# Rotary rotation on one core: the crossed rows fetched by small transfers instead of multiplied by a permutation matrix

## The chip, the cores and the metric

One core of one Trainium2 chip runs the whole kernel in one launch. The metric is the device time of an execution in microseconds (us); lower is better. The kernel before took 1447.31 us as the median of three runs.

## The reference, cut to what matters

Two stacks are computed in fp32 for 256 tokens of width 1024: first two layers of feed-forward blocks with a recurrent and a spatial gating mixer, then two "hybrid" layers of 272 tokens (16 meta tokens ahead) with windowed attention beside an mLSTM. Only this part of the hybrid layer bears on the change:

```python
aq, ak, av, ag, mq, mk, mv, mi, mf, mo, mgate = jnp.split(h @ w_in, split_points(), axis=-1)
q = rms_norm_2(aq.reshape(B, L, 16, 64), q_norm_g)      # 16 query heads of 64
k = rms_norm_2(ak.reshape(B, L, 2, 64), k_norm_g)       # 2 key heads of 64
q, k = apply_partial_rope(q, cos, sin), apply_partial_rope(k, cos, sin)

def apply_partial_rope(x, cos, sin):                    # half = 8: 16 of the 64 channels are turned
    x1, x2, rest = x[..., :half], x[..., half:16], x[..., 16:]
    return jnp.concatenate([x1 * c - x2 * s, x2 * c + x1 * s, rest], axis=-1)
```

## The kernel before, in words

**Layout.** Activations lie with channels on the 128 partitions (rows) and tokens along the row. A tile of queries is two heads, rows 0 to 63 and 64 to 127; there are eight of them (`q`), and one tile of keys (`k_att`). The rotation crosses rows 0 to 7 of each head with its rows 8 to 15.

**Weights.** All weights are streamed once in units of 512 KB (`UNITS`). SP issues the transfer of a unit into one of four buffers `raw` (L541) once DVE has split the unit four before it; ACT rounds it into `w_hi` (L1128), DVE subtracts to get `w_lo` (L1866), and PE multiplies three ways (L691). For every fifth unit of the hybrid layers the two parts lie in `y_both` instead. ACT and DVE run four units ahead of PE there.

**The stream of a hybrid layer.** Its input products are 50 units, counted u = 0, 1, ...: kv (0, 1), mif (2, 3), aq (4 to 11), mqk (12 to 19), then mv, mo, ag, mg. Units 4 + 2i and 5 + 2i give query tiles 2i and 2i + 1. The table `VISITS` says what else belongs to a unit: PE does these steps behind the unit's products, DVE in its turn for the same unit, ahead of or behind the split of the unit four on. All of it is written out in one fixed order on each engine. ACT copies each raw query tile out of the bank (L1453) and squares it (L1464). PE then sums the squares of a head (`turn`, L924, at units 5, 6, 8, 10, 12).

**The rotation before.** POOL multiplies the raw tile by the sine table into `qs` (L1828) and by the cosine table into `qc` (L1829); both have two buffers. PE multiplies `qs` by `rot_g`, a signed permutation scaled by the norm's gains (`turned`, L934, in fp32: two passes, so two records, for one product; at units 5, 8, 10, 12, 14). DVE adds the bank and `qc` and writes the tile back in place (L2316, `q_ready`). POOL waits for that sum two tiles later. There are nine tiles in each of the two layers. The tables `cos_g` and `rot_g` are made by DVE (`tables`, L2261 to L2264) behind unit 1.

**After it.** At unit 16 PE transposes values (`kx`), and at unit 18 attention begins: PE scores a head (L994, L995) after DVE has taken the maximum of the head before it (L2358 to L2363, `s_max`), and so on for 18 items.

**Start.** SP issues four units, the meta tokens, and then one small transfer for each parameter vector (L530, L534), before the loop that issues unit 4 and on. PE waits for these parameters (`par_loaded`) behind its fourth unit.

```python
for _c in range(9):
    VISITS[5 if _c == 0 else 6 + 2 * ((_c - 1) // 2)].append(("turn", _c))
for _c in range(9):
    VISITS[5 if _c == 0 else 8 + 2 * ((_c - 1) // 2)].append(("turned", _c))
```

## Time and profile before

| | us |
|---|---|
| runs, median (lowest to highest) of three | 1447.31 (1446.77 to 1447.53) |
| profiled execution, its own time | 1446.78 |
| its span | 1445.0 |
| busy in the span: PE, DVE, ACT, POOL | 1429.0, 1094.9, 853.8, 272.9 |
| first hybrid layer, kv to mqk | about 909 to 981 |
| second hybrid layer, kv to mqk | about 1178 to 1247 |

The profile is one execution. Times of events are us from the span's start. Busy time says that an engine had an instruction in it; the matmuls are pipelined and their ends are modelled, so intervals between starts are used for PE. The chain of waits goes back from the last instruction, at each step to what released it or to the instruction before it on its engine.

### The profile page before, as it was taken

To read this page: it belongs to the slowest core of one execution; us is meant where nothing else is said; L and a number is where in the kernel's file an instruction comes from. 1 tells how busy PE (TensorE), PEld (TensorE's weight loads), DVE (VectorE), ACT (ScalarE), POOL (GpSimd) and SP (SyncE) were. 2 spreads that over 40 slices of the span, in tenths; PEclk is the share of its full clock that TensorE was granted. 3 is DMA by queue.
4 is the path that set the end of the run, shared out by engine and by line. 5 is a ranking of instruction groups with operands and counts; after the bars stand their busy time and mean duration, and the time that the engine had idled before them with its cause. 6 is when DMAs were issued, how large, how long until landed. Compare 5 with 4: busy or idle time off the path is not lost.

```text
span 1445.0 us, 27301 instructions
## 1 busy us (share of the span) xinstructions
PE 1429.0 (99%) x9633; PEld 1318.0 (91%) x9633; DVE 1094.9 (76%) x2031; ACT 853.8 (59%) x1559; POOL 272.9 (19%) x329
## 2 busy tenths in 40 slices
PE   8999999999999999999999999999999999999998
PEld 7888899988888888889988888999999999999998
DVE  6777679877766777667787766798878779986883
ACT  6665458766544656446566655656757555576762
POOL 1111113121102111014031113332250035121000
PEclk9999999999999999999999999999999999999999
DMA  6667754556655666565456655554344555434533
GB/s 213 197 193 211 234 179 132 183 182 202 183 190 182 190 188 195 183 196 169 155 171 201 186 189 173 163 144 126 92 125 137 171 148 160 126 102 122 148 116 121
DMA packets 247876, 241.25 MB, mean 167 GB/s; under 512 B 15457, under 2 KB 246737, under 8 KB 247785
## 3 DMA queue, kind: packets, MB, share of 16 engines
q1 hardware_dynamic: 244888, 236.73, 53.6%
q10 hardware_dynamic: 2896, 3.30, 0.8%
q8 instruction: 58, 0.95, 0.3%
q14 instruction: 34, 0.27, 0.1%
HBM read 238.92 MB, written 1.07 MB: 166 GB/s over the span
## 4 chain that ended last, share of the span: by engine, by line
PE 79%; DVE 13%; ACT 5%; issue 2%; DMA 1%; ACTq 0%; SPq 0%; DVEq 0%
PE bank L691 72%; DVE w_lo L1866 3%; ACT w_hi L1128 1%; DVE work L2474 1%; DVE work L2423 1%; DVE work L1903 1%; PE bank L1011 1%; DVE y_both L1866 1%; PE bank L995 1%; ACT L1160 1%; DMA raw<-in_ffn_w_in_dram 1%; DVE work L2497 1%; PE bank L978 1%; PE bank L1012 0%; PE bank L994 0%
## 5 line engine op out<-in xcount | busy, mean ns | idle before, releaser
L691 PE MATMUL bank<-x_both,w_hi 128*128 128x512 f32 (+2 forms) x3216 | 747.5, 336 | 1.3 <-DVE w_lo L1866 0.8
L1866 DVE TENSOR_TENSOR w_lo<-raw,w_hi 128x1024 fp32r<-128x1024 f32 (+1 forms) x429 | 519.4, 1234 | 203.2 <-ACT w_hi L1128 202.2
L1128 ACT CAST w_hi<-raw 128x1024 fp32r<-128x1024 f32 (+1 forms) x429 | 429.4, 1028 | 125.2 <-PE bank L691 108.0
L691 PEld LDWEIGHTS bank<-x_both,w_hi 128*128 128x128 f32 x3216 | 467.5, 189 | 4.1 <-DVE w_lo L1866 1.6
L691 PEld LDWEIGHTS bank<-x_both,w_lo 128*128 128x128 f32 x2312 | 405.6, 188 | 62.5
L691 PE MATMUL bank<-x_both,w_lo 128*128 128x256 f32 (+1 forms) x2312 | 461.9, 281 | 0.0
L691 PE MATMUL bank<-y_both,w_hi 128*128 128x512 f32 (+2 forms) x1376 | 331.5, 342 | 1.6 <-DVE w_lo L1866 1.0
L691 PEld LDWEIGHTS bank<-y_both,w_lo 128*128 128x128 f32 x1040 | 184.3, 188 | 31.3
L691 PE MATMUL bank<-y_both,w_lo 128*128 128x256 f32 (+1 forms) x1040 | 206.1, 280 | 0.0
L691 PEld LDWEIGHTS bank<-y_both,w_hi 128*128 128x128 f32 x1376 | 200.2, 189 | 2.5 <-DVE w_lo L1866 1.4
L1753 POOL TENSOR_TENSOR work<-work,rstd 128x256 f32<-128x256 f32 x88 | 66.9, 782 | 412.7 <-ACT work L1197 412.7
L1179 ACT COPY pre<-bank 128x256 f32<-128x256 f32 x176 | 56.9, 375 | 67.1 <-PE bank L691 66.9
L1209 ACT CAST y_both<-work 128x256 f32 (+1 forms) x88 | 32.7, 406 | 59.5 <-DVE work L1934 59.4
L691 PE MATMUL bank<-x_both,y_both 128*128 128x272 f32 (+1 forms) x504 | 67.6, 290 | 0.0
L1197 ACT ACTIVATE work<-work 128x256 f32<-128x256 f32 x88 | 33.2, 418 | 53.3 <-DVE work L1923 53.3
L691 PEld LDWEIGHTS bank<-x_both,y_both 128*128 128x128 f32 x504 | 63.6, 188 | 0.6
L1139 ACT ACTIVATE x_both<-h,par 128x256 fp32r<-128x256 f32 (+1 forms) x56 | 28.2, 514 | 60.6 <-DVE h L1979 52.9
L1814 POOL TENSOR_SCALAR work<-work 128x256 f32<-128x256 f32 x32 | 36.3, 1135 | 95.6 <-DVE work L2391 95.6
L1718 POOL TENSOR_TENSOR sq<-h 128x256 f32<-128x256 f32 (+1 forms) x34 | 21.4, 629 | 163.2 <-DVE h L1979 162.9
L1883 DVE SCALAR_TENSOR_TENSOR x_both<-h,par,x_both 128x256 fp32r<-128x256 f32 (+1 forms) x56 | 29.1, 529 | 24.8 <-ACT x_both L1139 24.7
L1941 DVE TENSOR_TENSOR y_both<-work,y_both 128x256 f32 (+1 forms) x88 | 33.6, 423 | 15.3 <-ACT y_both L1209 14.7
L1903 DVE TENSOR_TENSOR work<-bank,rstd 128x256 f32<-128x256 f32 (+1 forms) x98 | 37.5, 422 | 4.5 <-PE bank L691 4.2
(312 smaller groups left out, 1395.7 us busy)
## 6 DMA issues: line engine op xcount, KB each, us to landing
raw<-in_ffn_w_in_dram SPq DMA_DIRECT2D x176, 512.0 KB, 3.8
raw<-in_w_in_dram SPq DMA_DIRECT2D x100, 512.0 KB, 3.7
raw<-in_ffn_w_out_dram SPq DMA_DIRECT2D x64, 512.0 KB, 4.6
raw<-in_w_out_dram SPq DMA_DIRECT2D x32, 512.0 KB, 4.5
raw<-in_ffn_w_out_dram SPq DMA_DIRECT2D x32, 384.0 KB, 3.4
raw<-in_rec_w_in_dram SPq DMA_DIRECT2D x16, 512.0 KB, 4.3
raw<-in_sg_w_in_dram SPq DMA_DIRECT2D x16, 512.0 KB, 4.3
raw<-in_rec_w_out_dram SPq DMA_DIRECT2D x8, 512.0 KB, 3.5
```

The lines of the kernel that those rows point to most:

```text
L691: i_ = mm(accs[m][:, cols], w[:, j, m * P:(m + 1) * P], moving, start=begin and g == 0 and not residual, stop=final)
L1128: nc.scalar.copy(hi_part(U)[:, 0:n, :], raw[:, s, 0:n, :]).then_inc(hi_made, 1)
L1139: i_ = activation(xview(dst, k, N), src, ACT.Copy, scale=scale)
L1179: nc.scalar.copy(ffn_b[:, m, :], bank[b][:, SEQ:2 * SEQ]).then_inc(low_copied, 1)
L1197: activation(ffn_s[:, m, :], ffn_t[:, m, :], ACT.Silu).then_inc(silu_done, 1)
L1209: nc.scalar.copy(dst, ffn_h[:, m, :]).then_inc(act_hi, 1)
L1753: TT(ffn_r[:, m, :], ffn_s[:, m, :], rstd[:, META:L], MUL).then_inc(gate_scaled, 1)
L1814: TS(pr[:, P:AW], pr[:, P:AW], rec[:, 1:2], None, MUL).then_inc(s_prob, 1)
L1866: TT(lo_part(U)[:, 0:n, :], raw[:, s, 0:n, :], hi_part(U)[:, 0:n, :].bitcast(fp32), SUB).then_inc(lo_made, 1)
L1883: i_ = STT(out=xview(dst_lo, k, N), in0=src, scalar=scale, in1=hi, op0=MUL, op1=SUB)
L1903: TT(dst, tile(pr, m, N), rstd[:, T0:L], MUL).then_inc(tile_read, 1)
L1941: TT(lo, ffn_h[:, m, :], hi.bitcast(fp32), SUB).then_inc(act_ready, 1)
```

## The change

PE's product with `rot_g` is gone, and so is `rot_g` (and the constant `rot`). The crossed rows come from transfers inside SBUF: SP copies rows 8 to 15 of each head onto rows 0 to 7 of another tile, and rows 0 to 7 onto rows 8 to 15. That takes four transfers for the key tile and four for each pair of query tiles, 20 in a layer. They stand in SP's queue ahead of the weight loads of units 9, 13, 15, 17 and 19 (`CROSS_AT`), each set behind a wait until ACT has read the tiles out. The targets are buffers that are free at that time (`mv` for queries, the last tile of `qk` for keys). POOL waits for the four transfers and multiplies the crossed tile by `sin_g`, a table of 272 columns which has the sign and the crossed gains in it; DVE's sum takes both operands from SBUF and waits for POOL. The crossed gains come by six more parameter transfers at the start.

```diff
-WORK_SLOTS = 67
+WORK_SLOTS = 69
...
-            c["sin"][h0 + k:h0 + k + half] = np.sin(ang)
+            c["sin"][h0 + k:h0 + k + half] = np.sin(ang) * (1 if k else -1)
...
+CROSS_AT = {9: 4, 13: 0, 15: 1, 17: 2, 19: 3}
...
-        rot_g = region(2, P)
+        sin_g = region(2)
...
+        crossed_k, crossed_q = qk[:, NC8 - 1, :], mv
...
+                half = ROT // 2
+                for n, src in (("attn_q_crossed", attn_q_norm_g_2), ("attn_k_crossed", attn_k_norm_g_2)):
+                    t, r, k = PAR[n]
+                    both = par_rows[r:r + k, t, :].rearrange("l (e d) -> l e d", e=2)
+                    for a, b, w in ((0, half, half), (half, 0, half), (ROT, ROT, DH - ROT)):
+                        g = src[:, b:b + w].rearrange("l (o d) -> l o d", o=1).broadcast_to((k, 2, w))
+                        sp.dma_start(both[:, :, a:a + w], g).then_inc(par_loaded, 16)
...
+            def cross(l, i):
+
+                half, T0 = ROT // 2, META if l == DEPTH - 1 else 0
+                cols = slice(2 * i, 2 * i + 2)
+                src, dst = (k_att, crossed_k) if i == 4 else (q[:, cols, T0:L], crossed_q[:, cols, T0:L])
+                sp.wait_ge(tile_read, 2 * PHASES[f"kv{l}"][1] + 1 if i == 4 else 2 * (PHASES[f"aq{l}"][1] + i) + 2)
+                for a in (0, DH):
+                    for x, y in ((a, a + half), (a + half, a)):
+                        sp.dma_start(dst[x:x + half], src[y:y + half]).then_inc(crossed[i], 16)
...
+                        if src == "w_in_2" and U - PHASES[f"kv{l}"][0] in CROSS_AT:
+                            cross(l, CROSS_AT[U - PHASES[f"kv{l}"][0]])
...
-                pe.wait_ge(par_loaded, 16 * 17)
+                pe.wait_ge(par_loaded, 16 * 23)
...
-                def turned(c):
-
-                    n = 9 * l + c
-                    pe.wait_ge(qc_new, n + 1)
-                    pe.wait_ge(cos_ready, l + 1)
-                    if c >= 2:
-                        pe.wait_ge(q_ready, n - 1)
-                    mm(bank[5 + n % 2][:, 0:L], rot_g[:, 0 if c else 1, :], qs[:, n % 2, :], start=True,
-                       stop=True).then_inc(rot_mm, 1)
...
-                do = dict(turn=turn, turned=turned, rt=rt, kx=lambda n: kx(), att=att,
+                do = dict(turn=turn, turned=lambda n: None, rt=rt, kx=lambda n: kx(), att=att,
...
-                    TT(qs[:, n % 2, :], src, cst("sin"), MUL)
+                    pool.wait_ge(crossed[(c - 1) // 2 if c else 4], 64 * (l + 1))
+                    TT(qs[:, n % 2, :], crossed_q[:, c - 1, :] if c else crossed_k, sin_g[:, 0 if c else 1, :], MUL)
...
-                    TS(rot_g[:, 0, :], cst("rot"), gq, sc, MUL, MUL)
-                    TS(rot_g[:, 1, :], cst("rot"), gk, None, MUL).then_inc(cos_ready, 1)
+                    TS(sin_g[:, 0, :], cst("sin"), pcol("attn_q_crossed", l), sc, MUL, MUL)
+                    TS(sin_g[:, 1, :], cst("sin"), pcol("attn_k_crossed", l), None, MUL).then_inc(cos_ready, 1)
...
-                    dve.wait_ge(rot_mm, n + 1)
-                    TT(dst, bank[5 + n % 2][:, 0:L], qc[:, n % 2, :], ADD).then_inc(q_ready, 1)
+                    dve.wait_ge(qc_new, n + 1)
+                    TT(dst, qs[:, n % 2, :], qc[:, n % 2, :], ADD).then_inc(q_ready, 1)
```

PE's queue behind unit 8 of the first hybrid layer, before (L924 sums the squares of a head, L934 is the product with `rot_g`, L691 the products of the next unit):

```order
L924 MATMUL bank<-con,work 128x2 [waits qsq_new]
L924 MATMUL bank<-con,work 128x2
L924 MATMUL bank<-con,work 80x2
L934 MATMUL bank<-work 128x272 [waits cos_ready,qc_new]
L934 MATMUL bank<-work 128x272 [waits q_ready,cos_ready,qc_new]
L691 MATMUL bank<-x_both,y_both 128x272 [waits lo_made]
```

and the same place now (the same lines have other numbers in the changed file, L944 and L711):

```order
L944 MATMUL bank<-con,work 128x2 [waits qsq_new]
L944 MATMUL bank<-con,work 128x2
L944 MATMUL bank<-con,work 80x2
L711 MATMUL bank<-x_both,y_both 128x272 [waits lo_made]
L711 MATMUL bank<-x_both,y_both 128x272 x23
```

Two products and their three kinds of waits have gone from between the sums and the next unit; nothing has come in their place.

SP's queue in the first hybrid layer now, from unit 4's load on (L549 are weight loads, L576 the crossing transfers; before, there were weight loads alone):

```order
L549 DMA raw<-in_w_in_dram 128x4x256 [waits lo_made] x5
L576 DMA work<-work 8x272 [waits tile_read]
L576 DMA work<-work 8x272 x3
L549 DMA raw<-in_w_in_dram 128x4x256 [waits lo_made] x4
L576 DMA work<-work 8x544 [waits tile_read]
L576 DMA work<-work 8x544 x3
L549 DMA raw<-in_w_in_dram 128x4x256 [waits lo_made] x2
L576 DMA work<-work 8x544 [waits tile_read]
L576 DMA work<-work 8x544 x3
L549 DMA raw<-in_w_in_dram 128x4x256 [waits lo_made] x2
```

Each set of four, and its wait for ACT's reading of the tiles, now stands ahead of a weight load.

DVE's queue in its turn for units 7 and 8 of the first hybrid layer, now (L1877 is the split, L2045 a 4-row step of the gates, L2327 the sum that was L2316 and waited for `rot_mm`):

```order
L2045 SCALAR_TENSOR_TENSOR work<-work 4x272 [waits dch] x3
L1877 TENSOR_TENSOR w_lo<-raw,w_hi 128x1024 [waits hi_made,dch]
L2327 TENSOR_TENSOR work<-work 128x272 [waits qc_new] x2
L1877 TENSOR_TENSOR w_lo<-raw,w_hi 128x1024 [waits hi_made]
L2045 SCALAR_TENSOR_TENSOR work<-work 4x272
```

Nothing has moved here; the sums read `work` alone where they read a bank and `work`, and wait for POOL in place of PE.

## Rows read from the trace of the kernel before

**Rows 1.** The page's busy time of each engine.

```profile
PE 1429.0 (99%) x9633; PEld 1318.0 (91%) x9633; DVE 1094.9 (76%) x2031; ACT 853.8 (59%) x1559; POOL 272.9 (19%) x329
```

**Rows 2.** Timeline of PE: start, length, line, shape, count; around two steps behind a unit.

```profile
931.70 0.75 PE L691 MATMUL bank<-x_both,w_hi 128*128 128x272 f32 x4
932.29 0.42 PE L691 MATMUL bank<-x_both,w_lo 128*128 128x272 f32 x2
...
1221.19 1.16 PE L934 MATMUL bank<-work 128*128 128x272 f32 x4
...
1222.70 0.42 PE L691 MATMUL bank<-x_both,w_lo 128*128 128x272 f32 x2
```

**Rows 3.** Chain of waits, first hybrid layer: start, length, what.

```profile
917.55 1.86 DVE rstd L1888
...
995.61 0.49 PE bank L994 x2
```

**Rows 4.** Chain of waits, second hybrid layer.

```profile
1232.83 0.45 DVE pre L1903
...
1261.69 0.49 PE bank L994 x2
```

**Rows 5.** DVE's waits for PE, 1182 to 1262: us in total, times, longest.

```profile
DVE pre L1903 <- PE bank L691: 0.7, 2, 0.4
...
DVE work L2316 <- PE bank L934: 0.4, 1, 0.4
```

**Rows 6.** Timeline of DVE: the tables, one of 272 and one of 128 columns.

```profile
920.06 0.36 DVE L2262 TENSOR_SCALAR work<-con,par 128x272 f32<-128x272 f32 x1
...
920.53 0.28 DVE L2264 TENSOR_SCALAR work<-con,par 128x128 f32<-128x128 f32 x1
```

**Rows 7.** By source line, 913 to 975 (split) and 900 to 1000 (sum): ns min/median/max.

```profile
L1866 DVE TENSOR_TENSOR w_lo<-raw,w_hi x15: 1204/1224/1693, 914.2 to 974.6; 128x1024 fp32r<-128x1024 f32 x15
...
L2316 DVE TENSOR_TENSOR work<-bank,work x9: 420/433/441, 934.7 to 965.3; 128x272 f32<-128x272 f32 x9
```

**Rows 8.** The start: SP, ACT, DVE and PE's timelines, and two answers on transfers.

```profile
13.21 0.55 SPq L534 DMA_DIRECT2D par_rows<-in_attn_k_norm_g_dram  x2
14.14 45.41 SPq L541 DMA_DIRECT2D raw<-in_ffn_w_in_dram  x18
...
DMA to landing us min/median/max: 3.6/3.6/3.6
...
L569 SPq DMA_DIRECT2D sink_tail<-in_attn_sink_dram x32: 341/484/1406, 127.2 to 166.8; - x32
...
16.34 2.94 ACT L1128 CAST w_hi<-raw 128x1024 fp32r<-128x1024 f32 x3
...
24.30 0.75 DVE L1918 TENSOR_TENSOR work<-bank,pre 128x256 f32<-128x256 f32 x2
...
25.73 0.70 PE L691 MATMUL bank<-x_both,w_hi 128*128 128x512 f32 x2
```

**Rows 9.** First hybrid layer: first pair read, loads landing (927 to 932), POOL's products, first sums.

```profile
928.58 0.79 ACT L1453 COPY work<-bank 128x272 f32<-128x272 f32 x2
...
DMA to landing us min/median/max: 3.6/4.3/4.6
...
L1828 POOL TENSOR_TENSOR work<-work,con x9: 662/672/1515, 922.1 to 959.1; 128x272 f32<-128x272 f32 x9
...
L1829 POOL TENSOR_TENSOR work<-work x9: 769/1737/1753, 923.6 to 959.7; 128x272 f32<-128x272 f32 x9
...
941.37 0.78 DVE L2316 TENSOR_TENSOR work<-bank,work 128x272 f32<-128x272 f32 x2
```

**Rows 10.** Timelines around the load of unit 19: issue, last pair read, its cast.

```profile
950.70 0.37 SPq L541 DMA_DIRECT2D raw<-in_w_in_dram  x1
...
951.15 0.81 ACT L1453 COPY work<-bank 128x272 f32<-128x272 f32 x2 [3.93 <-PE bank L691]
...
962.93 1.04 ACT L1128 CAST y_both<-raw 128x1024 fp32r<-128x1024 f32 x1
```

More of the change, by code:

```diff
@@ L36 @@
 C_AQ, C_KV, C_AG, C_MQK, C_MV, C_MIF, C_MO, C_MG = 0, 1024, 1280, 2304, 3328, 4352, 4360, 5384
-CONST_W = dict(ident=P, tri=P, amask=AW, tmask=L, mmask=P, rot=P, head_mean=2, cos=L, sin=L, k_rows=P, tail_rows=P, tail_head=ATT_H)
+CONST_W = dict(ident=P, tri=P, amask=AW, tmask=L, mmask=P, head_mean=2, cos=L, sin=L, k_rows=P, tail_rows=P, tail_head=ATT_H)
 CONST_AT = {}
@@ L61, in constants @@
     half = ROT // 2
-    for h0 in (0, DH):
-        for d in range(half):
-            c["rot"][h0 + half + d, h0 + d] = -1
-            c["rot"][h0 + d, h0 + half + d] = 1
     c["head_mean"][i, i // DH] = 1.0 / DH
@@ L87 @@
     [("norm_g_2", 16), ("mlstm_conv_w_2", 64), ("mlstm_conv_b_2", 16), ("mlstm_out_norm_g_2", 16),
-     ("attn_q_norm_g_2", 2), ("attn_k_norm_g_2", 2)],
+     ("attn_q_norm_g_2", 2), ("attn_k_norm_g_2", 2), ("attn_q_crossed", 2), ("attn_k_crossed", 2)],
 ]):
@@ L444, in build_stack @@
             sem(n) for n in ("ws_tr", "ws_read", "vt_tr", "vt_read", "sg_mm", "sg_read"))
-        cos_ready, qsq_new, qc_new, turn_mm, rot_mm, q_ready = (
-            sem(n) for n in ("cos_ready", "qsq_new", "qc_new", "turn_mm", "rot_mm", "q_ready"))
+        cos_ready, qsq_new, qc_new, turn_mm, q_ready = (
+            sem(n) for n in ("cos_ready", "qsq_new", "qc_new", "turn_mm", "q_ready"))
+        crossed = [sem(f"crossed{i}") for i in range(5)]
         rs_new, rt_mm, rt_read, k_ready, tail_new = (
```

## The prediction, on record before the changed kernel ran

> **What bounds the kernel now.** I read the busy table first: PE is busy for 99% of the span, DVE for 76% [rows 1]. By that table alone every microsecond taken off PE would come off the kernel. PE's waits are short everywhere, so the table can't tell whether PE is the bound or only never idle; the chain of waits can. In the first hybrid layer the chain is on DVE from 917.55 (the reciprocal) to 995.61, where it goes over to PE's score product L994 [rows 3]. Between these two rows stand 113 pieces of DVE, 19 of ACT and its queue, and none of PE. DVE works almost without a gap there: splits, gates, convolution, rotation sums. PE has split units ready ahead of it, so it is always busy too, but what it does has no bearing on DVE's next step. At 995.61 it has caught up and waits for DVE's maximum. All nine rotation products of that layer lie inside this stretch.
>
> In the second hybrid layer it is otherwise. The chain is on PE until about 1232.8, and on DVE and ACT from there to 1261.69, where it goes over to L994 again [rows 4]. Ahead of 1232.8 DVE is almost as full as in the first layer: its waits for PE between 1182 and 1262 are three, 0.7 us before two convolution steps and 0.4 us before one rotation sum [rows 5]. These 1.1 us are all that DVE can be ahead of its old time when PE comes sooner. Behind them PE waits for DVE.
>
> **What PE loses.** Without rotation products the first two tiles' products of a unit take 0.59 us from the first L691 behind L924 (931.70) to the first w_lo product (932.29). With two rotation products ahead it is 1.51 us from 1221.19 to 1222.70 [rows 2]. Two products cost 0.92 us, one 0.46. 18 products are 8.3 us of PE's time, 4.1 in each layer.
>
> **What comes of it.** In the first layer: nothing. The products lie beside DVE's full stretch [rows 3], DVE waits for none of them, and PE would reach the first score up to 4.1 us sooner and wait there for DVE. What is late next is what was late before, DVE. In the second layer: 1.1 us, DVE's own waits for PE [rows 5]. The bounds are 0 (other waits take their place) and 4.1 (all of it). I take 1.1, since each of the waits is on a PE step that comes sooner, and nothing beyond them can make a full DVE faster.
>
> **What DVE gets.** The tables: two of 128 columns become 272 wide, 0.36 against 0.28 us [rows 6]. That is 0.16 us a layer on the engine that is the bound, +0.3 in all. The sums: same shape, both operands in SBUF. In nine samples the sum from a bank took 420 to 441 ns, while the split, whose two operands lie in SBUF, took from 1204 to 1693 ns [rows 7]; the long ones stand where POOL was at its products. So a sum may be stretched as a split is, by up to 0.49 us. Four sums of nine are exposed in a layer: the key's, and the second of each pair that POOL's next product follows (there is none behind the last pair). The upper bound is 8 x 0.49 = 3.9 us. The other way, POOL's first query products come some 4 us later than before and stop stretching the steps that they now meet; two of those at 0.49 us a layer is the gain's bound, -2.0. I take 0: POOL is released by the first sum of a pair and arrives when the second has already begun. The Trainium skill (SBUF — State Buffer, Who interferes with whom) says that a VectorE instruction with two SBUF inputs contends with a GpSimd instruction that reads SBUF, that one with at most one SBUF input does not, and that who starts first is not the one that is held. The trace agrees with the first half of it. By that half alone the term would be as much as +3.9; by the second half, which no row shows apart, it would be 0.
>
> **What SP gets in the stream.** Four transfers at a time. The nearest row for an issue is L534, two in 0.55 us, so 0.3 with the gap; the median of another small kind is 0.484, 0.52 with the gap [rows 8]. Four take 1.2 to 2.1 us. They also hold the queue until ACT has read the pair. The worst place is unit 19: its load went out at 950.70, the pair is read at 951.96, so it goes out at 953.2 to 954.1, up to 3.4 us late. With 4.6 us to land, the longest of [rows 9], it is there by 958.7, and its cast begins at 962.93 [rows 10]. The other loads are held less. Cost 0; the cover is 4.2 us at that unit.
>
> **The crossing's own latency.** The key's transfers go out long before DVE's tables are made, and POOL waits for these anyway. The first query pair matters: read at 929.37, needed by DVE's second sum at 941.72 (each of the two sums takes half of 0.7) [rows 9]. Between lie four issues (1.2 to 2.1), the landing (3.6 to 4.6 by weight loads, since they queue behind two of those; a row for SBUF to SBUF there is none), and POOL's two pairs of products (0.67 + 1.74 = 2.4 each at the medians, 3.3 at the longest) [rows 9]. That is 9.6 to 13.3 us in 12.35: between 2.7 us of room and 0.9 us of wait. I take 0. Later pairs have more room, because POOL waits for DVE's sums of two tiles earlier there.
>
> **The start.** Six more parameter transfers stand ahead of the loop that loads unit 4. At 0.3 us each that load goes out 1.8 us later than 14.14. It landed in 3.6, at 17.74; ACT began its cast, the third of the three from 16.34, near 18.2, so 0.5 us is absorbed. The square root, DVE's reciprocal and the sums L1918 follow on that cast; the sums ended at 25.05 and PE's second product of unit 4 came at about 25.9 [rows 8], another 0.9 us. What is left is +0.4 us; at 0.52 an issue it would be +1.7, and the least is 0.
>
> **Sum.** -1.1 (second layer) + 0.3 (tables) + 0.4 (start) = -0.4 us. The profiled execution took 1446.78, the median is 1447.31, 0.5 above it. Against the execution this gives 1446.4, against the median **1446.9 us**.
>
> **The rivals.**
>
> *PE pays in full.* The busy table speaks for it [rows 1], the chain of the first layer against it [rows 3]. 8.3 us less, 0.4 for the start: 1439.4. The Trainium skill (Perfetto Trace Analysis, Identifying the Most-Contended Engine) says to take the engine of highest occupancy first, with a warning that matmul busy time is a poor measure; read plainly it names TensorE, and this would be the result. Chance 0.04.
>
> *Only the second layer pays in full.* For it: the chain is on PE for its first 50 us [rows 4]. Against it: DVE's waits there come to 1.1 us [rows 5]. 1447.3 - 4.1 + 0.2 + 0.4 = 1443.8. Chance 0.06.
>
> *The crossing comes late, and DVE waits.* The place is the first query pair in each layer. If a small transfer takes two landings of the longest kind, 9.2 us, because two weight loads stand in the same queue, then with 1.2 for the issues and 4.8 for POOL the second sum waits until 944.6, 2.9 us late, in each layer: 1446.9 + 5.8 = 1452.7. It decides from a landing of 6.3 us on. Against it: SP's and the queue's rate, 3.6 to 4.6 for 512 KB [rows 9]. Chance 0.05.
>
> *POOL holds the sums.* The stretch of 0.49 us on four sums a layer, 3.9 in all: 1450.8. For it: the splits are held [rows 7]. Against it: who comes first. It makes the kernel slower by more than the bound below from seven held sums of eight on. Chance 0.06.
>
> The forecast has 0.79.
>
> **How the numbers follow.** A measurement can tell some 0.2%, 2.9 us, from no change. The forecast's case lies inside that, but for a small part on either side (0.01 below, 0.03 above, where start, sums and crossing are all near their upper bounds). Faster: 0.04 + 0.06 + 0.01 = 0.11. Slower: 0.05 + 0.06 + 0.03 = 0.14. Same: 0.75. The range goes from 1444.7 (1446.9 with all of the -2.0 on the sums, and rounded out) to 1450.0 (the start at its upper bound, +1.3, and DVE's sums at somewhat under half of theirs); it leaves out the first two rivals and the ends of the last two.
>
> **What would show it.** Right: L934's records are gone and PE's busy sum is lower by some 8 us or PE waits more; the chain of the first layer stays on DVE from the reciprocal to a score product, at the same distance (78.1 us, within 0.5); PE's wait for DVE's maximum, 0.5 us before, is about 4 us around the first scores of each layer; in the second layer the distance from the reciprocal to that hand-over is about 1 us shorter; the six issues at the start take about 1.8 us. Wrong: a DVE sum that waits for POOL, sums of over 0.5 us, ACT's casts that wait for a weight load between units 13 and 19, or a first layer that gets shorter by more than 1 us.

## The result, and the profile after

| | before | the change |
|---|---|---|
| median, 20 executions each (lowest to highest), us | 1447.43 (1446.0 to 1448.97) | 1449.67 (1447.97 to 1451.46) |
| profiled execution, its own time, us | 1446.78 | 1448.66 |
| its span, us | 1445.0 | 1446.8 |

The ratio is 1.0015, 95% interval 1.0009 to 1.0021: 2.2 us slower. That lies inside my range (1444.7 to 1450.0) and within the 0.2% that I called no change, but the forecast was 0.4 us faster and the interval excludes that. The profiled execution lost 1.88 us, less than the median did. In all the runs of this document one execution stands apart from the others of its kernel (4980.53 us, in e18); no ratio uses it.

The page's busy time after [rows 1 before]:

```profile
PE 1423.1 (98%) x9597; PEld 1312.3 (91%) x9597; DVE 1096.2 (76%) x2031; ACT 852.8 (59%) x1559; POOL 273.1 (19%) x329
```

PE is busy for 5.9 us less by this table and the kernel isn't faster: PE waits instead. PE's waits for others between 917 and 1000, in total, times, longest:

```profile
PE bank L1004 <- DVE work L2366: 2.0, 1, 2.0
PE bank L1001 <- issue: 1.3, 1, 1.3
PE bank L958 <- DVE work L2311: 1.1, 1, 1.1
PE bank L1004 <- DVE work L2374: 0.5, 1, 0.5
```

Together these are 4.9 us. Before, PE had one wait in this stretch:

```profile
PE bank L994 <- DVE work L2363: 0.6, 1, 0.6
```

The removed products (4.1 us a layer) have become 4.3 us more of standing still, as forecast. The chain of waits in the first hybrid layer, the two rows that answer to [rows 3]:

```profile
918.41 1.86 DVE rstd L1899
...
997.32 0.49 PE bank L1004 x2
```

The chain stays on DVE, but the distance is 78.91 us and was 78.06: DVE itself got slower by 0.85 us. Where it got slower shows in two timelines of the change, POOL's and DVE's, of the first two query pairs:

```profile
936.19 0.79 POOL L1839 TENSOR_TENSOR work<-work 128x272 f32<-128x272 f32 x1 [10.72 <-ACT work L1463]
936.94 1.75 POOL L1840 TENSOR_TENSOR work<-work 128x272 f32<-128x272 f32 x1
938.65 0.97 POOL L1839 TENSOR_TENSOR work<-work 128x272 f32<-128x272 f32 x1
939.59 0.96 POOL L1840 TENSOR_TENSOR work<-work 128x272 f32<-128x272 f32 x1
943.10 0.80 POOL L1839 TENSOR_TENSOR work<-work 128x272 f32<-128x272 f32 x1 [2.56 <-DMA work<-work]
```
```profile
935.12 2.94 DVE L1877 TENSOR_TENSOR w_lo<-raw,w_hi 128x1024 fp32r<-128x1024 f32 x2
937.99 3.31 DVE L2045 SCALAR_TENSOR_TENSOR work<-work 4x272 f32<-4x272 f32 x4
941.34 1.23 DVE L1877 TENSOR_TENSOR w_lo<-raw,w_hi 128x1024 fp32r<-128x1024 f32 x1
942.48 0.79 DVE L2327 TENSOR_TENSOR work<-work 128x272 f32<-128x272 f32 x2
943.18 1.80 DVE L1877 TENSOR_TENSOR w_lo<-raw,w_hi 128x1024 fp32r<-128x1024 f32 x1
```

The four steps of L2045 in the kernel before:

```profile
937.82 2.38 DVE L2034 SCALAR_TENSOR_TENSOR work<-work 4x272 f32<-4x272 f32 x4
```

And POOL's timeline in the kernel before:

```profile
929.02 0.67 POOL L1828 TENSOR_TENSOR work<-work,con 128x272 f32<-128x272 f32 x1 [4.67 <-ACT work L1453]
929.66 1.74 POOL L1829 TENSOR_TENSOR work<-work 128x272 f32<-128x272 f32 x1
935.30 1.51 POOL L1828 TENSOR_TENSOR work<-work,con 128x272 f32<-128x272 f32 x1 [3.90 <-DVE work L2316]
936.77 1.74 POOL L1829 TENSOR_TENSOR work<-work 128x272 f32<-128x272 f32 x1
941.95 0.66 POOL L1828 TENSOR_TENSOR work<-work,con 128x272 f32<-128x272 f32 x1 [3.44 <-DVE work L2316]
```

Two things differ. The first query product waits for the crossing and starts at 936.19 in place of 929.02, so that four products run back to back. (The view names ACT as what released it; ACT had been done since 930.5, and without the transfers, in e3 below, the product starts at 930.14.) And the sine product of a pair's first tile takes 0.79 to 0.85 us, where it took 0.66 to 0.67. DVE's sums (two in 0.79) are what they were. What is stretched is what stands beside POOL's products: splits (1.80, where one alone takes 1.22 and the same two took 1.69 and 1.62 before) and the steps of four rows, L2045, which take 0.43 us alone. Before, one of the four stood beside a product (2.38 us for the four), now it is three (3.31), two of them at 0.90.

Added up step by step against the kernel before, DVE's lateness grows in the first layer by 0.15 (tables) + 0.11 (a step beside POOL's key product) - 1.05 (the split and the step that the first pair used to hold) + 1.04 (those it holds now) + 0.66 (0.06 to 0.18 at each later product) = 0.9 us. In the second layer the same list gives 0.15 + 0.11 - 0.48 + 1.04 + 0.7, less 1.2 for DVE's waits for PE, which are gone as forecast: 0.3.

### The profile page after: what moved, and what is told of

Its sections match the earlier page's. It is cut to its first block, busy times and chain, and to the rows that moved or that the text cites. A ratio compares the mean times of both kernels' runs of the same rounds, so it can differ in the third digit from the quotient of the medians.

```text
span 1446.8 us, 27259 instructions
## 1 busy us (share of the span) xinstructions
PE 1423.1 (98%) x9597; PEld 1312.3 (91%) x9597; DVE 1096.2 (76%) x2031; ACT 852.8 (59%) x1559; POOL 273.1 (19%) x329
## 3 DMA queue, kind: packets, MB, share of 16 engines
HBM read 238.86 MB, written 1.07 MB: 166 GB/s over the span
## 4 chain that ended last, share of the span: by engine, by line
PE 76%; DVE 16%; ACT 4%; issue 2%; DMA 1%; ACTq 0%; DVEq 0%
PE bank L711 70%; DVE w_lo L1877 4%; DVE work L2434 1%; DVE work L2485 1%; DVE y_both L1877 1%; ACT w_hi L1138 1%; DVE work L1914 1%; PE bank L1021 1%; DVE work L2045 1%; PE bank L1005 1%; ACT L1170 1%; DVE work L2508 1%; PE bank L988 1%; DMA work<-in_x_dram 1%; DVE work L2327 0%
## 5 line engine op out<-in xcount | busy, mean ns | idle before, releaser
L711 PE MATMUL bank<-x_both,w_hi 128*128 128x512 f32 (+2 forms) x3216 | 747.6, 336 | 0.5 <-DVE h L1977 0.5
L1877 DVE TENSOR_TENSOR w_lo<-raw,w_hi 128x1024 fp32r<-128x1024 f32 (+1 forms) x429 | 520.5, 1236 | 203.1 <-ACT w_hi L1138 202.1
L711 PEld LDWEIGHTS bank<-x_both,w_hi 128*128 128x128 f32 x3216 | 467.6, 189 | 2.8 <-DVE w_lo L1877 0.6
L711 PEld LDWEIGHTS bank<-x_both,w_lo 128*128 128x128 f32 x2312 | 406.4, 189 | 62.7
L711 PE MATMUL bank<-x_both,w_lo 128*128 128x256 f32 (+1 forms) x2312 | 462.6, 281 | 0.0
L711 PE MATMUL bank<-y_both,w_hi 128*128 128x512 f32 (+2 forms) x1376 | 331.5, 342 | 1.4 <-DVE w_lo L1877 1.1
L711 PEld LDWEIGHTS bank<-y_both,w_lo 128*128 128x128 f32 x1040 | 184.3, 188 | 31.3
L711 PE MATMUL bank<-y_both,w_lo 128*128 128x256 f32 (+1 forms) x1040 | 206.1, 280 | 0.0
L711 PEld LDWEIGHTS bank<-y_both,w_hi 128*128 128x128 f32 x1376 | 200.3, 189 | 2.4 <-DVE w_lo L1877 1.3
L711 PE MATMUL bank<-x_both,y_both 128*128 128x272 f32 (+1 forms) x504 | 67.3, 289 | 0.0
L711 PEld LDWEIGHTS bank<-x_both,y_both 128*128 128x128 f32 x504 | 63.4, 188 | 0.4
```

What stands on the lines that cost most here:

```text
L711: i_ = mm(accs[m][:, cols], w[:, j, m * P:(m + 1) * P], moving, start=begin and g == 0 and not residual, stop=final)
L1877: TT(lo_part(U)[:, 0:n, :], raw[:, s, 0:n, :], hi_part(U)[:, 0:n, :].bitcast(fp32), SUB).then_inc(lo_made, 1)
```

## The experiments

To compare traced executions I use one measure throughout: how much later than in the kernel before PE begins a unit's products. An execution's own start differs by up to 0.8 us from that of the kernel before (unit 2), and that stays in all later numbers, so only differences between columns count.

| traced execution | unit 2 | unit 5 | ahead of first layer | behind it | ahead of second | behind it |
|---|---|---|---|---|---|---|
| the change | +0.35 | +0.90 | +0.86 | +1.72 | +1.58 | +1.88 |
| e1, no six transfers | -0.55 | -0.53 | -0.56 | +1.38 | +1.54 | +2.92 |
| e2, before with the six | +0.39 | +0.85 | +0.82 | +0.83 | +0.86 | +0.87 |
| e3, no crossing | +0.46 | +0.86 | +0.86 | +3.07 | +2.89 | +2.86 |
| e4, PE's work put back | +0.81 | +1.28 | +1.28 | +2.18 | +2.31 | +2.75 |
| e11, the change again | +0.37 | +0.72 | +0.65 | +2.69 | +3.17 | +3.47 |
| e5, waits filled | +0.14 | +0.65 | +0.64 | +1.54 | +1.67 | +2.13 |
| e6, and plain sine table | +0.78 | +1.12 | +1.07 | +1.25 | +1.02 | +0.88 |
| e13, and tables shifted | +0.58 | +1.02 | +1.03 | +0.49 | +0.16 | -0.66 |
| e18, shifted, not filled | +0.59 | +1.03 | +1.00 | +1.54 | +2.16 | +2.18 |
| e14, all edits | +0.38 | +0.38 | +0.39 | -1.12 | -1.32 | -3.11 |

(For the change and e5 the unit 2 entry is that of ACT's cast, since PE began it late for another reason; in the others both agree within 0.02.)

**The start: e1 and e2.** e1 takes the six parameter transfers out of the change (the sine tables take the uncrossed gains):

```diff
-                half = ROT // 2
-                for n, src in (("attn_q_crossed", attn_q_norm_g_2), ("attn_k_crossed", attn_k_norm_g_2)):
...
-                        sp.dma_start(both[:, :, a:a + w], g).then_inc(par_loaded, 16)
...
-                    TS(sin_g[:, 0, :], cst("sin"), pcol("attn_q_crossed", l), sc, MUL, MUL)
+                    TS(sin_g[:, 0, :], cst("sin"), gq, sc, MUL, MUL)
```

> The change without the six crossed-gain transfers at the start (the sine tables then take the uncrossed gains, so these are left out of the computation). Theory (of the change's +2.2 us some 0.9 is the start: unit 4's load goes out behind six issues of 0.26 to 0.30 us each): 0.9 us less than the change, 1448.8, and the first product of unit 5 at the same place as before within 0.2 us of the start's own jitter. Rival (the start's shift is a difference between executions, earlier rows differ too): no less than the change, 1449.7. Rival (my forecast's term): 0.4 less, 1449.3.

e2 adds the same six to the kernel before, where nothing reads them.

> The kernel before with only the six parameter transfers added, nothing reads them. Theory: +0.9 us against before, 1448.3, all of it in place by unit 5. Forecast's term: +0.4. Rival (jitter): 0.

Measured: e1 1449.51 (ratio 1.0013, 1.0004 to 1.0022), e2 1447.62 against 1447.34 (1.0001, 0.9992 to 1.0010). Both fall short of my theory of 0.9. The table shows why: of the 0.90 us at unit 5, 0.35 were there at unit 2, ahead of the six. From unit 2 to unit 5 the traced kernels with the six, at their place in the change, lose 0.35 to 0.55 us, those without lose 0.0. So the term of the forecast, +0.4, was right, and the theory that I formed from one trace was not. The medians alone couldn't have told: e2's 0.28 us more lies inside its uncertainty. SP's timeline of the change has the price of an issue, 0.29 us:

```profile
14.30 0.86 SPq L542 DMA_DIRECT2D par_rows<-in_attn_q_norm_g_dram  x3
15.20 0.86 SPq L542 DMA_DIRECT2D par_rows<-in_attn_k_norm_g_dram  x3
```

e1 also brought the first sign of something else. It lost 1.94 us in the first layer, where the change had lost 0.86, although it has less to do. By the windows of PE in e1 (length, busy time and count, granted clock, DMA share, GB/s):

```profile
960.00:975.00 15.00, 13.79 (x108) 1.00 0.41 115
975.00:981.00 6.00, 3.89 (x27) 1.00 0.50 155
981.00:987.00 6.00, 6.00 (x36) 0.72 0.40 116
```

**No crossing: e3.** POOL reads the uncrossed tile, nothing is transferred (so the crossing is left out):

```diff
-                        if src == "w_in_2" and U - PHASES[f"kv{l}"][0] in CROSS_AT:
-                            cross(l, CROSS_AT[U - PHASES[f"kv{l}"][0]])
...
-                    pool.wait_ge(crossed[(c - 1) // 2 if c else 4], 64 * (l + 1))
-                    TT(qs[:, n % 2, :], crossed_q[:, c - 1, :] if c else crossed_k, sin_g[:, 0 if c else 1, :], MUL)
+                    TT(qs[:, n % 2, :], src, sin_g[:, 0 if c else 1, :], MUL)
```

> The change without the 20 crossing transfers in the stream and without POOL's wait for them; POOL multiplies the uncrossed tile by the sine table, so the crossing is left out of the computation. Theory (the transfers make POOL's first query pair of a layer run back to back with the second, beside DVE's splits and forget-gate steps: 1.0 us more there, against 1.05 us less in the first layer and 0.48 us less in the second where the pair stood before): about 0.6 us less than the change, 1449.1. What remains above before (start 0.9, tables, a sine product of 0.80 to 0.85 us in place of 0.67) is not from the transfers. Rival (the transfers carry the whole loss, on SP or on POOL): back to 1447.4 or below, 2.2 us less.

Measured: 1449.53 (1.0015, 1.0006 to 1.0024). The theory was 1449.1, and the rival that the transfers carry the whole loss is out: without them it is as large. POOL's first pair is back at 930.14 and holds a split and a step again (+1.17 on DVE against the change), the two later steps are free again (-0.93). Both moves of the first pair that I had added up, -1.05 and +1.04, are real and cancel. In the second layer the table has 0.33 us less without the transfers, less than the 0.6 of the theory. This trace too has a stretch at a lower clock, from 982 to 986, and DVE waits 1.01 us for PE behind it.

**PE's work put back: e4.** 18 products of 272 columns on constants, at the old places, with no reader (the hook that calls `turned` is put back with it):

```diff
+                def turned(c):
+
+                    pe.wait_ge(cos_ready, l + 1)
+                    mm(bank[5 + (9 * l + c) % 2][:, 0:L], ident, cst("cos"), start=True, stop=True)
```

> The change with PE's 18 products of 272 columns put back at their old places, on constants, with no reader: PE's time alone is given back (8.3 us). Theory (PE's time is free in the first hybrid layer, worth 1.1 us in the second): 1450.8, the first layer's length unchanged within 0.2 us, DVE's waits for PE in the second layer back. Rival (PE pays in full): 1458.0. Rival (PE's time is free in both layers): 1449.7.

Measured: 1449.45 (1.0016, 1.0007 to 1.0025), no more than the change, and not the 1450.8 of the theory. This rules out the first two rivals of the prediction. By the table 8.3 us of PE's work cost 0.03 us in the first layer (0.89 against 0.86) and 0.14 in the second (0.44 against 0.30), so the second layer's 1.1 us did not come back either. With DVE later by POOL's holds, PE's old pace no longer made it wait. One caution on the medians: these products also shorten PE's longest wait, from 2.0 us to 0.7, and what such a wait can cost is the next point.

**The clock: e11 and e5.** e11 is the change once more, unaltered.

> The change once more. Theory (clock): 1449.6 median; in the traced execution either no stretch at 1.2 GHz and a time of 1448.6, or one or two, each right behind the 2.0 us wait of PE ahead of the second score product and each 1.05 us longer on DVE. Rival: 1.2 GHz stretches in other places, or a time above 1449.3 with none.

Measured: 1449.30 (1.0014, 1.0005 to 1.0023). Its traced execution took 1450.26 and has one stretch at a lower clock. PE's timeline there, and DVE's wait behind it:

```profile
982.05 0.80 PE L1004 MATMUL bank<-work 128*128 128x128 f32 x2 [1.99 <-DVE work L2366]
982.64 1.06 PE L1005 MATMUL bank<-work 128*128 128x256 f32 x2
983.14 1.47 PE L711 MATMUL bank<-x_both,w_hi 128*128 128x272 f32 x4
984.41 0.66 PE L711 MATMUL bank<-x_both,w_lo 128*128 128x272 f32 x2
984.86 0.95 PE L711 MATMUL bank<-x_both,w_hi 128*128 128x272 f32 x4
985.65 0.42 PE L711 MATMUL bank<-x_both,w_lo 128*128 128x272 f32 x2
```
```profile
DVE work L2369 <- PE bank L1005: 1.0, 1, 1.0
```

The same places in the change's first trace:

```profile
982.22 0.49 PE L1004 MATMUL bank<-work 128*128 128x128 f32 x2 [2.00 <-DVE work L2366]
982.54 0.60 PE L1005 MATMUL bank<-work 128*128 128x256 f32 x2
982.79 0.85 PE L711 MATMUL bank<-x_both,w_hi 128*128 128x272 f32 x4
983.48 0.41 PE L711 MATMUL bank<-x_both,w_lo 128*128 128x272 f32 x2
```

In both traces PE has stood still for 1.1 us ahead of 961, 1.3 ahead of 976 and 2.0 ahead of 982. Then, in some executions, the granted clock is the lower of its two levels, 1.2 GHz in place of 2.4, for some 3 us; the products take up to 1.7 times as long (1.47 for 0.85), the next score is ready 1 us late, and DVE, which has no slack there, waits for it. The layer costs 2.04 us here and 0.86 in the first trace. Seven traces of this study have the wait of 2.0 us, once in each layer, 14 in all; behind eight of the 14 stands such a stretch (two in e1, one in e3, one here, two in e12, two in e18; none in the change's first trace and in e9). In e12 and e18 it comes without the wait of 1.1 us. Where the wait of 2.0 us is shorter or missing, in eight traces of the changed form and five of the kernel before's, there is none in the hybrid layers. The Trainium skill (TensorE: Matmul & The Clock Gate, Part 1: The HAM clock gate) says that the clock of the array is at half its rate when it has been idle and that the point where it changes varies from run to run. These traces have the same two levels and the variation; but PE was at work on either side of the waits here, and none was longer than 2.0 us.

e5 fills the waits with products that nobody reads:

```diff
+                    for _ in range({0: 2, 1: 4}.get(v, 0)):
+                        mm(bank[6][:, 0:L], ident, cst("cos"), start=True, stop=True)
                     if v < len(ITEMS):
```

> The change with six products of 272 columns a layer on PE, on constants, into a bank that nobody reads then: two ahead of the first score product and four ahead of the second, in the places where PE waited 1.3 and 2.0 us. They give PE 2.8 us more work a layer and keep it from standing still. Theory (clock: in the first trace of the uncrossed and of the six-less kernel the granted clock falls to 1.2 GHz for some 4 us right behind the 2.0 us wait, and DVE then waits 1.0 us for PE's score; most executions of the change have one or more such stretches, its first traced one had none): the median falls by about 1.0 us to 1448.7, the slowest execution to under 1450.0, and the granted clock stays at 2.4 GHz around the first scores. Rival (the median lies above the traced execution by chance, the filling only costs): 1449.7 or more, up to 1452.

Measured: 1449.32 (1.0014, 1.0005 to 1.0023), from 1448.37 to 1450.08. PE's waits there are 0.4 and 0.2 us where they were 1.3 and 2.0, and the granted clock stays up:

```profile
PE bank L1003 <- issue: 0.4, 1, 0.4
PE bank L1006 <- DVE work L2368: 0.2, 1, 0.2
```

But the theory's gain of 1.0 us is not there. The median is 0.35 below that of the change's 20 executions and level with e11's (1449.30), and e11's slowest, 1450.26, is near e5's. The table shows a price of the filling too: e5 loses 1.37 us over both layers, 0.2 more than the change's first trace. So the filling is not shown to make the change itself faster; the pairs e10 and e12, e13 and e18 below are the ones where it counts.

**The sine product: e6, e9, e15, e13.** e6 is e5 with POOL's sine product on the plain table of the constants (gains and query scale are left out of the sine half):

```diff
-                    TT(qs[:, n % 2, :], crossed_q[:, c - 1, :] if c else crossed_k, sin_g[:, 0 if c else 1, :], MUL)
+                    TT(qs[:, n % 2, :], crossed_q[:, c - 1, :] if c else crossed_k, cst("sin"), MUL)
```

> The kernel with the filled waits, and POOL's sine product reads the plain sine table of the constants, in place of the table made from gains (so the crossed gains and the query scale are left out of the sine half). Theory (the sine product takes 0.80 to 0.86 us in place of 0.67 because of the place of its table, and each pair of products holds DVE 0.1 to 0.2 us longer, some 0.6 us a layer): sine products of 0.67 us again, and 1.0 to 1.2 us less than the filled kernel, 1447.6. Rival (it is the place of the crossed tile or another thing): 0.80 to 0.86 us as before, and 1448.7.

Measured: 1447.75 (1.0007, 0.9998 to 1.0016), 1.6 us below e5, a little more than expected. Each sine product is shorter by some 0.10 us, and so is the step of DVE that waits for its end. In the table the first layer gains 0.7 and the second 0.6 us against e5. This is the largest piece of the loss. Was it the allocation, the contents, or the place? e9 gives the tables their own allocation:

```diff
+        tab = sb("tab", [P, 4, L])
...
-        cos_g = region(2)
-        sin_g = region(2)
+        cos_g, sin_g = tab[:, 0:2, :], tab[:, 2:4, :]
```

> The change with the cosine and sine tables in an allocation of their own behind the constants, in place of slots of the large work allocation; nothing else. Theory (a product whose operands lie in two allocations takes 0.67 us alone and 0.75 behind a sum, one with all in the work allocation 0.77 and 0.85): both products of a pair get shorter by 0.1 us, DVE is held less by as much at each, some 0.7 to 1.2 us a layer: 1447.5 to 1448.3. Rival (the sine product was faster because it read the constants themselves, not because of the allocation): products as in the change, 1449.7.

Measured: 1449.91 (1.0017, 1.0008 to 1.0026), products of 0.76 and 0.85 us. The theory fell. e15 keeps that allocation, with the waits filled, and makes the sine tables by multiplying with 1.0 (so gains and query scale are left out of the sine half again):

> The kernel with the filled waits, tables in their own allocation and not shifted, and the sine tables made by multiplying the constants by 1.0, so that the sine product reads the same numbers as with the plain table (gains and query scale are left out of the sine half). Theory (place): sine products 0.76 and 0.85 as in the change, 1449.3. Rival (contents): 0.67 and 0.75, 1447.8.

Measured: 1448.97 (1.0012, 1.0003 to 1.0021), sine products still 0.76 and 0.85. So it isn't the contents. e13 shifts both tables by two columns:

```diff
+        tab_all = sb("tab", [P, 4 * L + 2])
+        tab = tab_all[:, 2:2 + 4 * L].rearrange("p (c n) -> p c n", n=L)
```

> The kernel with the filled waits (1449.3), with the cosine and sine tables in their own allocation and shifted by two columns (8 bytes) in it. The plain sine table, which POOL read fast, lies 1314 columns into the constants, 8 bytes off the 64-byte grid on which every tile of the work allocation lies. Theory (place in the grid: three operands at the same place in it make POOL's product 0.1 us longer): both products of a pair 0.67 us alone in place of 0.76, the first behind a sum 0.75 in place of 0.85, DVE held 0.1 us less by each: 1447.3 to 1448.0. Rival (something about the constants' contents or their allocation): 0.76 and 0.85 as before, 1449.3.

Measured: 1446.20 (0.9996, 0.9987 to 1.0005), 3.1 us below e5 and more than the 1.3 to 2.0 expected. It is the place. POOL and DVE by line and form between 930 and 962, e5 first, e13 second (busy us, mean ns):

```profile
L1841 POOL TENSOR_TENSOR work<-work 128x272 f32<-128x272 f32 x8 | 7.2, 903 | 19.3 <-DMA work<-work 10.5 <-DVE work L2329 8.8
L1842 POOL TENSOR_TENSOR work<-work 128x272 f32<-128x272 f32 x8 | 10.9, 1358 | 0.0
...
L2047 DVE SCALAR_TENSOR_TENSOR work<-work 4x272 f32<-4x272 f32 x7 | 6.0, 856 | 0.2
```
```profile
L1842 POOL TENSOR_TENSOR work<-work,tab 128x272 f32<-128x272 f32 x8 | 6.4, 798 | 19.3 <-ACT work L1466 10.5 <-DVE work L2330 8.8
L1843 POOL TENSOR_TENSOR work<-work,tab 128x272 f32<-128x272 f32 x8 | 10.1, 1262 | 0.0
...
L2048 DVE SCALAR_TENSOR_TENSOR work<-work 4x272 f32<-4x272 f32 x7 | 5.4, 769 | 0.2
```

Every product is 0.10 us shorter, and every step of DVE that waits for one to end is 0.10 to 0.11 us shorter, one after another, some 15 of them in the first layer. Sine and cosine product both gain, though the cosine product had this price in the kernel before too. A correction to the expectations: counted from the code, the operands in the work allocation all start on a multiple of 32 bytes from its beginning (three of them not on one of 64), the plain sine table 8 bytes off. Where the allocations themselves begin is not on record, and two more columns may move those behind them; but e6 changed the operand alone and moved nothing, and its sine products became as short. What size of grid counts, no run here shows.

**What the whole is worth: e10, e12, e14, e7, e16, e17, e18.** Since DVE is the bound, two more edits take work off it and off the start: POOL makes the tables (it was idle then), and unit 4's load goes ahead of the last small parameters.

```diff
-                        tables()
...
+                    if c == 0:
+                        tables()
                     pool.wait_ge(tile_read, 2 * PHASES[f"kv{l}"][1] + 1 if c == 0 else 2 * PHASES[f"aq{l}"][1] + c)
...
+                between()
                 for n, src in (("attn_q_norm_g_2", attn_q_norm_g_2), ("attn_k_norm_g_2", attn_k_norm_g_2)):
```

In the kernel before the two edits gave nothing (e7), nor did the shift of its cosine table (e16):

> The kernel before, with the rotation's four tables a layer made by POOL, which is idle then, in place of DVE, and unit 4's load ahead of the last four parameter transfers. Theory (DVE is the bound there, its four table steps take 1.1 us a layer): DVE's steps behind the tables come 1.1 us sooner in each layer, the start up to 0.5 us sooner: 1444.7. Rival (POOL's table steps and the later key products stretch DVE's reciprocal and splits instead, or PE then waits and its clock falls): 1446.5 to 1448.

> The kernel before with its cosine table in an allocation of its own, shifted by two columns. Theory (place): the cosine product 0.67 us alone in place of 0.77, so POOL's pairs hold DVE 0.1 us less; little of it reaches the end, since DVE then waits for PE in both layers (as it did where its tables went to POOL, which gave nothing): 1446.9 to 1447.4. Rival (contents or allocation): the product 0.77 us as before, 1447.4.

Measured: e7 1447.32 (1.0000, 0.9991 to 1.0009), e16 1446.86 (0.9999, 0.9990 to 1.0008). In e7's first layer DVE is 1.1 us sooner behind the tables' place and ends 0.2 us sooner. Net 0.2 us go at once, beside POOL's later steps, and the other 0.7 where DVE now waits for PE, at rotation sums and convolution steps. Before, the two engines stood almost level; what one gives, the other takes. In the change, all with the filling but for e12, and with the tables in slots of `work` (e8) or in their own allocation (e10, e12):

> The change with the filled waits, the tables on POOL, and unit 4's load ahead of the last ten small parameter transfers. Theory: against the filled kernel 0.5 to 1.0 us at the start and 1.4 us for the tables in each layer: 1445.2, some 2 us below before and level with the kernel before with the same two edits. Rival (as for that one): 1447 to 1448.5.

> All edits together (filled waits, tables made by POOL, unit 4's load ahead of the last small parameters, tables in their own allocation). Theory: 1.4 to 2.4 us below the kernel without the own allocation (1446.2), 1444.3. Rival: 1446.2.

> The same as the kernel with all edits, without the six filling products a layer. Theory (clock): PE again waits 1.3 and 2.0 us or more ahead of the first two score products, some executions have stretches at 1.2 GHz; the median is 0.3 to 1.0 us above the filled one, the slowest execution over 1.5 us above its fastest. Rival (the fill does nothing): the same median within 0.2 us and the same spread.

Measured: e8 1446.17 (0.9995, 0.9986 to 1.0004), 3.1 us below e5 and 1.0 short of the theory; e10 1446.53 (0.9995, 0.9986 to 1.0004), so the allocation alone gives nothing here either; e12, the same without the filling, 1447.59 (1.0000, 0.9991 to 1.0009), with two stretches at 1.2 GHz in its trace and a DVE wait of 0.95 us behind each. The filling's median is 1.1 us better here, and the slowest execution is 1446.98 in place of 1449.18; the fastest are alike (1445.75 and 1446.25), as they would be if an execution without a stretch loses nothing.

> All edits together (filled waits, tables made by POOL, unit 4's load ahead of the last small parameters) with the tables shifted by two columns. Theory (place): 1.0 to 2.0 us below the same without the shift (1446.5), 1445.0, faster than before by 2.4. Rival: 1446.5.

> The kernel before (PE makes the rotation) with the edits that took the change to 1443.8, as far as they apply: tables made by POOL, unit 4's load ahead of the last small parameters, cosine table shifted by two columns. Theory (without them the two engines stand level before the change, and with DVE eased PE's 8.3 us of rotation products are the bound in the stream): 1446.5, so that the rotation by transfers is worth some 2.7 us once DVE is not held. Rival (the edits alone are the gain, wherever the rotation is made): 1444.0.

> The change with the tables in their own allocation, shifted by two columns, and nothing else: the sine product's term alone, and the waits of PE not filled. Theory: the traced execution, where no stretch at 1.2 GHz falls in it, 3 us below that of the change (1445.7), the median 1446.7, its slowest over 1.5 us above its fastest. Rival (the fill is needed for the gain): 1449.

Measured: e14, with the shift, **1443.84** (0.9976, 0.9966 to 0.9985), 3.3 us faster than before and 1.2 below the theory. e17, the kernel before with the edits that apply to it, 1447.31 (1.0000, 0.9991 to 1.0009): all of them together gave nothing there, and I had expected 0.8. So the rotation by transfers does pay, by 3.5 us, once the other edits have relieved DVE. e18, the shift alone in the change, 1448.13 (1.0003, 0.9994 to 1.0013; from 1446.27 to 1448.84). Its windows of PE:

```profile
981.00:987.00 6.00, 6.00 (x34) 0.72 0.40 113
1247.00:1253.00 6.00, 5.40 (x29) 0.72 0.35 102
```

and DVE's waits for PE between 917 and 1000, then between 1182 and 1275 (of these two the second, at 1274, is at the full clock, and e9 and e10 have it too):

```profile
DVE work L2370 <- PE bank L1006: 1.0, 1, 1.0
```
```profile
DVE work L2370 <- PE bank L1006: 1.9, 2, 1.0
```

This traced execution took 1448.66, e13's 1446.03. The two kernels differ in the six filling products a layer, which only add work, and their medians by 1.9. By the table e18 loses 1.1 us against e13 in the first layer and 0.8 in the second, each with its stretch, and 0.9 between the layers (e11 loses 0.5 there against its own first layer). That comes at one cast of a weight unit, for which ACT waits 1.78 us in e18 (until 1151.59), 1.77 in e11 and 0.76 in e13; why that wait is so uneven no run here tests. My expectation that no stretch would fall into e18's trace was wrong, and so was the median of 1446.7.

## Why the prediction was wrong, point by point

- **PE's products are hidden in the first layer: right.** The chain stayed on DVE, PE waits 4.9 us there where it waited 0.6, and its work put back cost 0.03 us (e4).
- **The second layer gains 1.1 us: not as a gain of its own.** DVE's waits for PE did disappear (some 1.2 us in DVE's list), but DVE was late by more from POOL's holds, which would have closed the same waits (e4: 0.14 us between the two). I added a gain on a wait and a loss on the engine that waits as if they were separate.
- **Tables +0.3, start +0.4: right.** 0.15 us a layer, and 0.35 to 0.55 from unit 2 to unit 5.
- **SP's hold and the crossing's latency 0: right for what they were costed by.** No cast waited for a load in units 13 to 19, and DVE never waited for POOL's products. The issues took 0.62 to 0.77 us each (one of the 40 took 1.20), more than the 0.3 to 0.52 that I took; the room covered it. But a transfer that isn't late still moved POOL's first pair by 7.2 us to where other steps of DVE stand.
- **POOL's and DVE's collisions, "I take 0": this is the step that failed.** I bounded it at -2.0 to +3.9. For the loss I looked only at the sums, which indeed aren't stretched (0.79 for two, before and after), and for the gain at the steps that the first pair leaves, not at those that it comes to stand beside. The term had two parts that I didn't cost. The moved pair: -1.05 + 1.04 in the first layer, -0.48 + 1.04 in the second, +0.55 in all. And the sine product, which I took at its old 0.67 us although the change gives it a new table: it is 0.10 us longer, and DVE with it, 1.3 us over both layers by e6. Together about +1.9 where the forecast had 0. My signs of being wrong (a sum that waits, a sum over 0.5 us, a cast that waits for a load) looked past these steps too, and none of them came.
- **A term that was missing: PE standing still.** I wrote that PE would wait some 4 us for DVE and gave it no price. In some executions the clock falls to 1.2 GHz behind it, and each time DVE waits about 1 us. The first traced execution has none, so a comparison of the two first traces (1.88) couldn't show it. What it adds to the median is open, as said next.

The sum of the measured pieces: start 0.45, in the stream 0.86 + 0.30 = 1.16, together 1.6 of the median's 2.2. That leaves some 0.6 to the clock and to chance between executions, as a difference and not measured by itself. The estimates of the clock's share don't agree: eight stretches behind 14 waits at about 1 us each make 1.1 us an execution, e5 against the change gives 0.35, and e5 against e11 nothing.

That the time lies inside my range says little for the forecast. The range reached so far up because I allowed for held sums, and no sum was held; and in the lists of DVE's lateness above 1.2 us less of waiting stand against 2.4 us of losses. The direction was missed, and so were two of the signs that I had named for being right: the first layer's distance of 78.1 us within 0.5 (it is 78.91), and a second layer shorter by 1 us (it is longer by 0.3).

Of the rivals, the one that POOL holds DVE came nearest, by another mechanism than it named: not the sums, but the steps between them. The Trainium skill (SBUF — State Buffer, Who interferes with whom) says that a VectorE instruction with two SBUF inputs contends with a GpSimd instruction that reads SBUF, and that the order of issue decides who blocks. Both halves agree with these traces: the sum that starts first keeps its 0.43 us and POOL's product behind it is 0.75 in place of 0.67 (e13), while a step of 0.43 us that starts behind a product's start ends 0.3 us behind its end (0.90 us at a product of 0.97, 0.79 at one of 0.86). I had used the rule on one kind of instruction and should have gone through all of DVE's steps beside POOL's new times.

What stays open: why the place of a table in its allocation changes POOL's time; how often the clock falls in an ordinary execution of the change; and what the cast between the layers waits for.

## What to carry to other kernels

When an operand of an instruction moves to another buffer, its duration need not be the one in the trace, and if another engine's instructions wait for its end, the difference counts once for each. Where one engine's work is removed while another is the bound, ask what its new waits do: in two of three pairs here (e10 and e12, e13 and e18, not the change and e5) the kernel with the waits filled by useless products was the faster one by its median. And before adding up gains and losses on two engines that stand nearly level, take the later of the two at each hand-over; the sum of both is neither.

## What the runs showed that I had not expected

- POOL's product of 128 x 272 takes 0.77 us with three operands that all start on multiples of 32 bytes in their allocation, and 0.67 us when one of them is shifted by 8 bytes (e13 against e5 and e9; in e16 the cosine product of the kernel before goes from 0.77 to 0.66 by the same shift). Behind a DVE sum it is 0.85 and 0.75.
- A small step of DVE (4 x 272, 0.43 us alone) that starts just behind a POOL product's start ends 0.3 us behind its end: its time changes one for one with POOL's.
- A waiting TensorE can cost the engine that it waits for: behind a wait of 2.0 us, with one of 0.5 to 1.3 us a few us ahead of it, the granted clock was at 1.2 GHz for some 3 us, and the score came 1 us late. It followed on eight of 14 such waits, and at the same places on none that was shorter.
- An issue of a crossing transfer took 0.62 to 0.77 us on SP in 39 of 40 cases, one of a parameter row 0.29.
